# Turning tiles on VectorE and through DRAM instead of on TensorE, in a hybrid HGRN2 and attention block

## What is computed

```python
h = rmsnorm(x, g_mix);  z = h @ w_in            # 2048 x 14848
q_r, f_r, i_r, og_r, q_a, k_a, v_a, gate_a, gate_b = split_columns(z)
o_a = hgrn2_mixer(q_r, f_r, i_r, og_r, ...)     # 16 heads of 128, chunks of 64
o_b = swa_sink_attention(q_a, k_a, v_a, ...)    # 32 heads of 64, band of 2 chunks, sinks
merged = concat(sigmoid(gate_a) * o_a, sigmoid(gate_b) * o_b)
x = x + merged @ w_out
x = x + square(relu(rmsnorm(x, g_mlp) @ w_up)) @ w_down
x = x + sigmoid(x @ w_ple_gate) * (p @ w_ple_proj)
return rmsnorm(x, g_final)
```

## Time and profile before

| | |
|---|---|
| median of 3 runs | 1716.85 us (1716.4 to 1717.51) |
| the profiled execution | 1718.0 us |
| its span | 1716.3 us |
| TensorE, VectorE, ScalarE busy | 99%, 64%, 54% |
| mean granted clock | 0.998 of full speed |
| DMA | 315.30 MB, mean 184 GB/s, 59.5% of the 16 engines by the weights' queue |

### The profile page before, as it was taken

How to read it: one execution, slowest core, us unless ns; L and a number is a source line. 1 busy time by engine, 2 the same in 40 slices (tenths; PEclk the granted TensorE clock), 3 DMA queues, 4 the chain that set the end, 5 groups by cost and what they waited for, 6 DMA issues and landing times.

```text
span 1716.3 us, 22351 instructions
## 1 busy us (share of the span) xinstructions
PE 1696.1 (99%) x8669; PEld 1416.6 (83%) x8669; DVE 1102.8 (64%) x1405; ACT 925.0 (54%) x1227; POOL 16.9 (1%) x72
## 2 busy tenths in 40 slices
PE   7999999999999999999999999999999999999997
PEld 6888888788887888878888888888888888888886
DVE  6667866875668756687585565656555556566565
ACT  6466647655565555655546554544444445454454
POOL 3000000000000000000000000000000000000000
PEclk9999999999999999999999999999999999999999
DMA  6655555556655566555556666666666665655554
GB/s 216 203 174 180 173 173 168 176 176 181 185 180 173 173 183 185 173 173 176 181 177 212 186 192 191 190 190 193 190 193 188 194 189 193 190 190 187 181 184 136
DMA packets 163292, 315.30 MB, mean 184 GB/s; under 512 B 10161, under 2 KB 10482, under 8 KB 163058
## 3 DMA queue, kind: packets, MB, share of 16 engines
q1 hardware_dynamic: 162016, 312.01, 59.5%
q10 hardware_dynamic: 1170, 1.87, 0.3%
HBM read 311.74 MB, written 2.10 MB: 183 GB/s over the span
## 4 chain that ended last, share of the span: by engine, by line
PE 98%; DVE 1%; ACT 1%; DMA 0%; issue 0%; SPq 0%; DVEq 0%; ACTq 0%
PE acc L678 22%; PE acc L679 22%; PE acc L684 22%; PE acc L692 6%; PE turn L692 6%; PE turn L678 3%; PE turn L679 3%; PE turn L684 3%; PE turn L698 3%; PE acc L698 3%; PE turn L720 2%; PE turn L747 0%; PE turn L771 0%; PE turn L820 0%; PE turn L759 0%; DMA w_raw<-in_w_in_dram 0%
## 5 line engine op out<-in xcount | busy, mean ns | idle before, releaser
L1334 DVE TENSOR_TENSOR w_lo<-w_raw,w_hi 128x1024 fp32r<-128x1024 f32 x588 | 720.0, 1224 | 562.9 <-ACT w_hi L977 560.2
L977 ACT ACTIVATE w_hi<-w_raw 128x1024 fp32r<-128x1024 f32 x588 | 622.7, 1059 | 700.7 <-PE acc L684 444.9
L678 PE MATMUL acc<-w_hi,hT 128*128 128x512 f32 x1104 | 435.6, 395 | 4.4 <-ACT w_hi L977 4.4
L679 PE MATMUL acc<-w_hi,hT 128*128 128x512 f32 x1104 | 431.1, 390 | 0.0
L684 PE MATMUL acc<-w_lo,hT 128*128 128x512 f32 x1104 | 296.2, 390 | 0.0
L678 PEld LDWEIGHTS acc<-w_hi,hT 128*128 128x128 f32 x1104 | 207.8, 188 | 48.4 <-ACT w_hi L977 5.6
L684 PEld LDWEIGHTS acc<-w_lo,hT 128*128 128x128 f32 x1104 | 207.8, 188 | 43.6
L679 PEld LDWEIGHTS acc<-w_hi,hT 128*128 128x128 f32 x1104 | 208.0, 188 | 41.9
L678 PE MATMUL acc<-w_hi,mT_hi 128*128 128x512 f32 x416 | 164.4, 395 | 0.0
L679 PE MATMUL acc<-w_hi,mT_lo 128*128 128x512 f32 x416 | 162.2, 390 | 0.0
L692 PE MATMUL acc<-hT,w_hi 128*128 128x512 f32 x448 | 140.0, 394 | 0.0
(11 more groups left out here) (247 smaller groups left out, 1545.7 us busy)
## 6 DMA issues: line engine op xcount, KB each, us to landing
w_raw<-in_w_in_dram SPq DMA_DIRECT2D x232, 512.0 KB, 3.7
w_raw<-in_w_up_dram SPq DMA_DIRECT2D x128, 512.0 KB, 3.8
w_raw<-in_w_down_dram SPq DMA_DIRECT2D x128, 512.0 KB, 4.3
w_raw<-in_w_out_dram SPq DMA_DIRECT2D x64, 512.0 KB, 3.8
w_raw<-in_w_ple_gate_dram SPq DMA_DIRECT2D x32, 512.0 KB, 4.6
x_sb<-in_x_dram SPq DMA_DIRECT2D x8, 256.0 KB, 7.4
w_raw<-in_w_ple_proj_dram SPq DMA_DIRECT2D x4, 512.0 KB, 3.7
out_dram<-x_sb SPq DMA_DIRECT2D x6, 256.0 KB, 3.1
```

Source lines behind the costliest of these rows:

```text
L678: pe.matmul(a, hi[:, k, t, :], w_hi[:, s, kk, :], start=first and kk == 0, stop=False)
L679: pe.matmul(a, lo[:, k, t, :], w_hi[:, s, kk, :], start=False, stop=False)
L977: act.activation(w_hi[:, n % W_SLOTS], w_raw[:, n % RAW_SLOTS], ACT.Copy)\
L1334: dve.tensor_tensor(w_lo[:, n % W_SLOTS], w_raw[:, n % RAW_SLOTS], w_hi[:, n % W_SLOTS].bitcast(F32), ALU.subtract).then_inc(w_lo_ready, 1)
```

## The change

- Six tiles per group are turned by VectorE (`turn_blocks`), each in two transposes: a 128x512 half of za, zb, sgb or the weights goes in blocks of 32x32 into `eg` or `eg2`, which alternate. SyncE stores the result in four DMAs of 32 partitions each, in runs of 1 KB, into a scratch tensor in DRAM, one per tile and group, and loads it back in one DMA, so that each block stands in its place. VectorE turns at steps -4 (qa), 9 (f), 10 (first weights), 17 (q), 20 (gate), 22 (second weights); SyncE stores 8 chunks later in its own count and loads 9 later. SyncE's load of chunk n waits for w_lo of chunk n - 4, and stores and loads of the turned tile come behind the weight load of their chunk.
- TensorE's turns of these tiles and VectorE's copies to pT are gone. Who read a turned bank now waits for the landing and reads SBUF. qT is copied at step 1 instead of -2.
- Steps: F_TURN from (9, 26) to (12, 29), Q_TURN from (17, 28) to (20, 32), DECAY from (20, 35) to (23, 35), KE_TURN from (25, 40) to (28, 40).
- The turned chunks go in pairs: the products with w_hi of both chunks, then those with w_lo of both.

```diff
-            pT = mb("pT", [P, 2, 4, P])
+            pT = mb("pT", [P, 4, 2, 4, 32])
...
+        TURNED = ("qa", "f", "p0", "q", "gb", "p1")
+        turned_rows = [nc.dram_tensor(f"turned_rows{i}", [P, 4, 256], F32, kind="Internal")
+                       for i in range(NG * len(TURNED))]
+        blocks = (eg, eg2)
+        def turn_number(kind, j):
+            return len(TURNED) * j + TURNED.index(kind)
+        def turned_block(tile, m0, nm):
+            return tile.rearrange("p b (m c) -> p m b c", c=32)[:, m0:m0 + nm]
+        def whole(tile):
+            return tile[:].rearrange("p t (b x) -> p (t b) x", b=2)
...
-                use(("qaT", j, t), t, qaT_out, 2 * j + t + 1)
-            for t in range(TT):
...
-                for g in range(2):
-                    use(("pT", j, t, g), g, pT_out, 2 * (2 * j + t) + g + 1)
...
-            for t in range(TT):
-                use(("gbT", j, t), t, am_ready, 2 * j + t + 1)
...
-                use(("fT", j, hp), 2, f_exp, 2 * j + hp + 1)
...
-                use(("qT", j, hp), 3, q_ready, 2 * j + hp + 1)
...
-        F_TURN, Q_TURN, DECAY, KE_TURN = (9, 26), (17, 28), (20, 35), (25, 40)
+        F_TURN, Q_TURN, DECAY, KE_TURN = (12, 29), (20, 32), (23, 35), (28, 40)
+        TURN_AT = {"qa": -4, "f": 9, "p0": 10, "q": 17, "gb": 20, "p1": 22}
+        TO_STORE, TO_LOAD = 8, 9
...
+        def by_blocks(tile):
+            return tile[:].rearrange("p (m b c) -> p m b c", m=4, b=4)
+        def by_tile(tile, t):
+            return turned_block(whole(tile), 0, 8).rearrange("p (k t) b c -> p t k b c", t=TT)[:, t]
...
+            def store_turned(kind, j):
+                i = turn_number(kind, j)
+                sp.wait_ge(blocks_turned, 2 * (i + 1))
+                rows_ = turned_rows[i].rearrange("(c i) b x -> b i c x", c=4)
+                for b in range(4):
+                    sp.dma_start(rows_[b], whole(blocks[i % 2])[32 * b:32 * b + 32]).then_inc(blocks_stored[i % 2], 16)
+            def load_turned(kind, j):
+                i = turn_number(kind, j)
+                if kind == "p0" and j:
+                    sp.wait_ge(full(("pv", j - 1, 1)), nth(("pv", j - 1, 1)))
+                if kind == "p1":
+                    sp.wait_ge(full(("pv", j, 0)), nth(("pv", j, 0)))
+                sp.wait_ge(blocks_stored[i % 2], 64 * (i // 2 + 1))
+                to, landed = {"qa": (whole(zb), qaT_landed), "f": (whole(za), fT_landed), "q": (whole(zb), qT_landed),
+                              "gb": (whole(sgb), gbT_landed)}.get(kind, (pT[:].rearrange("p b h k c -> p b (h k c)"),
+                                                                         pT_landed))
+                sp.dma_start(to, turned_rows[i][:]).then_inc(landed, 16)
...
+                for j in range(NG):
+                    for kind in TURNED:
+                        if slot[0] == A0[j] + TURN_AT[kind] + TO_STORE:
+                            store_turned(kind, j)
+                        if slot[0] == A0[j] + TURN_AT[kind] + TO_LOAD:
+                            load_turned(kind, j)
...
+                if turned(kind, j):
+                    if c % 2:
+                        turned_pair(n - 1, col, c - 1, last, r)
+                    return
...
-                if turned(kind, j):
-                    turned_chunk(n, col, c, s, first, last, r)
-                    return
...
-            def turned_chunk(n, col, c, s, first, last, r):
-                for kk in range(2):
-                    for ct in range(4):
-                        pe.matmul(turned_acc(col, ct)[:], w_hi[:, s, kk, ct * P:(ct + 1) * P],
-                                  hT[:, 2 * c + kk].rearrange("p a t c -> p (a t c)"),
-                                  start=first and kk == 0, stop=False)
-                pe.wait_ge(w_lo_ready, count(n + 1, r, LOOP_CHUNKS))
-                for kk in range(2):
-                    for ct in range(4):
-                        mm = pe.matmul(turned_acc(col, ct)[:, 0:TT * P], w_lo[:, s, kk, ct * P:(ct + 1) * P],
-                                       hT_hi[:, 2 * c + kk].rearrange("p t c -> p (t c)"), start=False,
-                                       stop=last and kk == 1)
-                mm.then_inc(w_used, 1)
+            def turned_pair(n, col, c, last, r):
+                for c_, s in ((c, n % W_SLOTS), (c + 1, (n + 1) % W_SLOTS)):
+                    pe.wait_ge(w_hi_ready, count(n + 1 + c_ - c, r, LOOP_CHUNKS))
+                    for kk in range(2):
+                        for ct in range(4):
+                            pe.matmul(turned_acc(col, ct)[:], w_hi[:, s, kk, ct * P:(ct + 1) * P],
+                                      hT[:, 2 * c_ + kk].rearrange("p a t c -> p (a t c)"),
+                                      start=c_ == 0 and kk == 0, stop=False)
+                for c_, s in ((c, n % W_SLOTS), (c + 1, (n + 1) % W_SLOTS)):
+                    pe.wait_ge(w_lo_ready, count(n + 1 + c_ - c, r, LOOP_CHUNKS))
+                    for kk in range(2):
+                        for ct in range(4):
+                            mm = pe.matmul(turned_acc(col, ct)[:, 0:TT * P], w_lo[:, s, kk, ct * P:(ct + 1) * P],
+                                           hT_hi[:, 2 * c_ + kk].rearrange("p t c -> p (t c)"), start=False,
+                                           stop=last and c_ > c and kk == 1)
+                    mm.then_inc(w_used, 1)
...
-            def head_turn(kind, j, hp, src):
-                turn((kind, j, hp), lambda i: src[:, i % 2, (2 * hp + i // 2) * P:(2 * hp + i // 2 + 1) * P])
...
-            def weights_turn(j, t, g):
-                name = ("pT", j, t, g)
-                pe.wait_ge(pn_ready, 2 * (2 * j + t) + g + 1)
+            def weighted_values(j, t):
+                name = ("pv", j, t)
+                pe.wait_ge(pT_landed, 16 * (2 * j + t + 1))
...
-                for i in range(4):
-                    hh, pair = i // 2, 2 * g + i % 2
-                    mm = pe.transpose(bank(name)[:, i * P:(i + 1) * P], pr[:, pair, hh, 0:P], ident[:])
-                mm.then_inc(full(name), 1)
-            def weighted_values(j, t):
-                name = ("pv", j, t)
-                pe.wait_ge(pT_out, 2 * (2 * j + t + 1))
-                signal, value = bank_free(name)
-                pe.wait_ge(signal, value)
-                parts_ = ((0, slice(0, P)),) if t == 0 else ((V_MIXED, slice(0, CHUNK)), (V_LATE, slice(CHUNK, P)))
-                for v, qs in parts_:
+                parts_ = ((0, slice(0, 4)),) if t == 0 else ((V_MIXED, slice(0, 2)), (V_LATE, slice(2, 4)))
+                for v, bs in parts_:
...
-                        mm = pe.matmul(four(bank(name)[hh * HD:(hh + 1) * HD, :])[:, :, qs], vv[:, v, j, :],
-                                       pT[:, hh, :, qs], start=True, stop=True, skip_group_check=True)
+                        out_ = bank(name)[hh * HD:(hh + 1) * HD, :].rearrange("p (k b c) -> p k b c", k=4, b=4)
+                        mm = pe.matmul(out_[:, :, bs], vv[:, v, j, :], pT[:, bs, hh].rearrange("p b k c -> p k b c"),
+                                       start=True, stop=True, skip_group_check=True)
...
-                    if a == -3:
-                        for t in range(TT):
-                            pe.wait_ge(qa_rotated, 2 * j + t + 1)
-                            turn(("qaT", j, t), lambda i: zb[:, t, i * P:(i + 1) * P])
...
-                        for g in range(2):
-                            if a == SCORES[t] + 7 + 2 * g:
-                                weights_turn(j, t, g)
...
-                    if a == ATT_END:
-                        for t in range(TT):
-                            pe.wait_ge(gb_sig, 2 * j + t + 1)
-                            turn(("gbT", j, t), lambda i: sgb[:, t, i * P:(i + 1) * P])
...
-                        if h == F_TURN[hp]:
-                            pe.wait_ge(f_out, 2 * (j + 1))
-                            head_turn("fT", j, hp, za)
-                        if h == Q_TURN[hp]:
-                            pe.wait_ge(q_out, 2 * (j + 1))
-                            head_turn("qT", j, hp, zb)
...
-                        act.wait_ge(pT_out, 2 * (2 * j + t))
+                        act.wait_ge(blocks_turned, 2 * (turn_number("p0" if t else "p1", j if t else j - 1) + 1))
...
-                    if a == -2:
-                        for t in range(TT):
-                            act.wait_ge(full(("qaT", j, t)), nth(("qaT", j, t)))
-                            act.activation(qT[:, :, t, :], four(bank(("qaT", j, t))[:]), ACT.Copy)\
+                    if a == 1:
+                        act.wait_ge(qaT_landed, 16 * (j + 1))
+                        if j:
+                            for hh in range(2):
+                                act.wait_ge(full(("score", j - 1, 1, hh)), nth(("score", j - 1, 1, hh)))
+                        for t in range(TT):
```

(61 more changed lines are left out.)

8 lines of the change are left out of this document (7 added, 1 removed).

## The result

The changed kernel takes 1735.12 us (median of 4, 1733.86 to 1737.16) against 1716.88 (1716.4 to 1717.51): 1.0107 times the time before, 95% interval 1.0093 to 1.012. It is slower by 18.2 us where 17 us less were forecast, and beyond the range, which ended at 1722.

What follows compares the result with a forecast made beforehand. TensorE, busy for 99% of the span, was taken to bound the kernel: 1718.0 - 22.2 - 1.1 + 6.0 = 1700.7, and with the median 1.15 below the profiled execution, 1700 us; range 1691 to 1722.

Steps and rivals of the forecast that it cites:

- term for waits: New TensorE waits in four groups: 0.9 us a group from the walk plus 0.6 for unwalked places, 6 us.
- the gain: 192 transposes leave TensorE as 48 groups of four, 32 alone at 0.47 us and 8 pairs at 0.90: 22.2 us.
- the pairs: Paired up-chunks halve TensorE's switches from narrow to wide products: 0.02 us for each of 56 pairs, 1.1 us gained.
- the products with runs of 32: TensorE's products with the weights read pT in runs of 32: no change, at worst 10 us.
- Block transposes: 48 block transposes of 128x512 added to VectorE, 0.69 us each, 20 us into its idle time.
- The third rival: VectorE's block transposes cost twice the price, 1.22 us each: 13 us more, 1713 us; chance 16%.
- Round trip: Turned tile through DRAM, from the weight load: stores landed after 5.2 us, load 3.8 more, 9.0 us; bounds 5.8 and 12.
- The walk: HGRN queries followed through a group's queues: w_lo(28) 0.2 us late, second weights 0.7 us late, 0.9 us a group.
- w_lo(28): VectorE's w_lo copy for chunk 28 of a group: ready at 31.9 us, wanted at 31.7, so 0.2 us late.
- ScalarE's waits: ScalarE's w_hi waits for landed tiles, 4 to 6 us, eight in all; none at the rotated queries.
- The slow one: Second rival: round trip too long, at SyncE's stores, f and q, and pT; 1728 us at 12 us; chance 17%.
- VectorE's order: A VectorE step waits for ScalarE's later exponentials, both queues stretch past product 40: 5 us a group, 1720 us; 5%.

Runs made afterwards that it cites:

- el_keys: The change with stores and loads one chunk earlier, weighted values three chunks later, second half of the recurrence and keys' scores two steps later: 1699.93 us, 0.9900 of the kernel before.
- filler: The change with 18 or 30 unread identity transposes on TensorE ahead of each wait for turned weights: 1727.59 us, 1.0057 of the kernel before.
- late: The change with the weighted values read three chunks later, at steps 19 and 31: 1720.59 us, 1.0021 of the kernel before.
- early_late: The change with stores and loads one chunk earlier and weighted values read three chunks later: 1707.86 us, 0.9943 of the kernel before.
- shifted: The change with stores and loads one chunk earlier, weighted values three chunks later, whole recurrence two steps later: 1719.18 us, 1.0016 of the kernel before.
- load_later: The change with SyncE's loads of the turned tiles 10 instead of 9 chunks behind the turn: 1761.99 us, 1.0262 of the kernel before.
- early: The change with SyncE's stores and loads at 7 and 8 chunks behind the turn, not 8 and 9: 1708.37 us, 0.9943 of the kernel before.

## Why the prediction was wrong

The sum failed at its term for waits, 1.5 x 4 = 6 us, where 25.1 were measured, and at a term that it didn't have, the clock, worth 10 to 14 us. Its other terms (the gain, the pairs, the products with runs of 32) held.

**The gain, 22.2 us.** Right: el_keys keeps the whole change on its engines and comes out at 1699.93; without the gain its sum would be 20 us too high.

**The pairs, 1.1 us.** Right in size (5.57 us a pair against 5.59), not resolved by the medians.

**The products with runs of 32**, at no change: right; 1.08 us for the group at full clock (341.87), as in the filler's run and in the kernel before.

**Block transposes, 0.69 us.** Right, from the row of the nearest form. VectorE's groups by form, the largest of four (the others have 687 to 691 ns):

```profile
L1497 DVE STREAM_TRANSPOSE eg<-zb 128x512 f32<-128x512 f32 x16 | 10.4, 691 | 0.1
```

The 128x512 float32 block transpose takes 0.691 us. The third rival (1.22) is out. The Trainium skill (VectorE: DVE Perf Modes, The three transpose paths) led to an estimate of 1.24 us from its bf16 figure; the measurement decides against it for this form.

**Round trip of 9.0 us: the term that was mis-sized.** In the second group it was 10.5 to 11.1, and 12.7 for the first weights. By parts, from the weight load's issue: the stores had landed after 5.7 to 5.8 us (5.2 forecast), the load took 4.7 to 5.4 more (3.8). The view of the stores' line, then that of the loads' line, say more:

```profile
L607 SPq DMA_DIRECT2D turned_rows<-eg x96: 302/460/1336, 78.6 to 771.8; - x96
...
DMA to landing us min/median/max: 2.7/3.9/7.0
```

```profile
DMA to landing us min/median/max: 3.2/4.3/5.3
```

One store's issue costs SyncE 0.46 us and up to 1.34, where the forecast had 0.35 from an output store, and never added up the four: 1.9 to 2.8 us pass until the last one is issued.

**The walk: the step that failed.** It followed q, w_lo(28) and the second weights, and put 0.6 us on "places that I did not walk". One of these was the first weights, turned at 10 and wanted at 16, one step behind f in the same SyncE list: 0.64, 3.84, 1.94 and 1.12 us of TensorE's waits, 7.5 in all, in no term. The second weights came late by (19.3 - 7.5) / 4 = 3.0 us a group against 0.7; 1.5 of that is the longer trip. w_lo cost 5.0 us against 0.8. Together 24.3 us in TensorE's waits, 25.1 by the windows, against 6.0.

**The clock: a term that was missing.** I took the 2.4 GHz of the earlier trace rows as given. Around TensorE's waits it fell to 1.2 GHz for 28 us more than before, which cost 10 to 12.5 us by filler, and 13.9 at most. Part of these 28 us lies in the waits themselves, where it costs nothing: before 170.37 and 782.33 the clock is down for the last 0.7 and 1.6 us of the wait.

**ScalarE's waits** of 4 to 6 us, eight of them: eight there were, of 6.7 us on average (53.5 / 8). Four more, at the rotated queries (7.1 us), were forecast to be none: 14.0 against 14.7 left 0.7 us, less than the 1.5 us by which the trip was longer. That w_hi would still be in time for TensorE was right.

**The rivals.** The slow one named the right places (SyncE at the stores, ScalarE at f and q, pT for product 28) but not the price: at the measured 10.5 us its own rule, two waits of 1.5 us a group, gives 1712 and no slower kernel, and 1735 came, for it left out the first weights and the clock. Its 28 us at 12 us also counts 1 us at w_hi(25) where 3 - 2.4 = 0.6 remain, 26 us. Its chance of 17% rested on "against it: the typical 3.8", a landing of one DMA alone. The section of the Trainium skill that it draws on (DMA: Bandwidth & Descriptors, Anatomy of one DMA) is on DMAs issued by GpSimd, while these were SyncE's, whose shortest store landed in 2.7 us. VectorE's order, the last rival, came true in part, though only in the altered kernels: in late, early_late and shifted TensorE waits for `ke` where it had waited elsewhere.

## What to carry to other kernels

When a tile leaves the bound engine for a trip through memory, list **every** reader with the time it asks and the time the trip lands, count the issue time of each of its DMAs, and look for trips that share a queue; a walk of one chain says nothing of the others. A wait on the bound engine may be paid twice, once as standing and once in the clock after it. Where the deadlines are the loss, move the trip and its readers, by a chunk or two, and look after each move for what is late next: here three such moves turned +1.1% into -1.0%, and a fourth, the whole recurrence two steps later (shifted), lost 11 us.

## What the runs showed of the hardware that was not expected

- Of TensorE's eight waits for pT in the changed kernel, six, of 1.9 to 3.8 us, have a stretch at 1.2 GHz at their end or right behind them: at 170.37 and 347.31 eight products take 1.98 us that take 1.08 in filler. The two of 0.6 and 1.1 us (132.19, 741.41) have none (1.08 us for four products). The length of the wait alone doesn't settle it. In load_later one of 2.1 us is not followed by it, while in early one of 1.39 us before 548.50, close behind one of 1.64 before 545.90, is (1.98 us for eight products). What decides between them stays open. The line of load_later:

```profile
319.59 1.08 PE L815 MATMUL turn<-pT,vv 128*64 128x512 f32 x4 [2.12 <-DMA pT<-turned_rows]
```

- Work that nobody reads, put in place of the wait, makes the kernel faster: 192 transposes, 21.5 us, for 7.5 us less.
- A 128 KB store's issue takes SyncE 0.302 to 1.336 us (median 0.460), the 512 KB load of a turned tile 0.343, all 24 times (0.344 at most); from GpSimd's list they take 0.550 and 0.565 (median), and land later.
